# Neighbourhood attention on Trainium2: unnormalised exponentials, the inverse sums spread by a product with the identity

## The reference

```python
q, k, v = jnp.split(h @ w_qkv, 3, axis=-1)            # 16 heads of 64
q, k = rms_norm_2(_heads(q), q_g), rms_norm_2(_heads(k), k_g)
# the same for the 256 context tokens: k_c, v_c
s_loc = einsum('bhrqd,bhrikd->bhrqik', qg, kg) * scale + bias    # 4 rows x 64 columns of the grid
s_loc = where(col_mask, s_loc, NEG_INF)
s_ctx = einsum('bhrqd,bhcd->bhrqc', qg, k_c) * scale
p = softmax(concatenate([s_loc, s_ctx], -1), -1)
o = einsum(p_loc, vg) + einsum(p_ctx, v_c)
x = x + g1 * (merge(o) @ w_o)
x = x + g2 * conv_ffn(modulate(x, ...), ...)
```

## Time and profile before

| | |
|---|---|
| timed runs | 1769.03, 1772.07, 1773.03 us |
| profiled execution, its own time | 1772.83 us |
| its span, first to last instruction | 1771.0 us |
| mean granted TensorE clock | 0.969 |
| busy, share of the span | TensorE 95%, weight loads 83%, VectorE 56%, ScalarE 42%, GpSimd 5% |
| neighbourhood attention, first scores to first product of the projection | 1464.09 to 1541.72 us |

### The profile page before, as it was taken

How to read it: one execution, slowest core, us unless ns; L and a number is a source line. 1 busy time by engine, 2 the same in 40 slices (tenths; PEclk the granted TensorE clock), 3 DMA queues, 4 the chain that set the end, 5 groups by cost and what they waited for, 6 DMA issues and landing times.

```text
span 1771.0 us, 29417 instructions
## 1 busy us (share of the span) xinstructions
PE 1677.8 (95%) x11903; PEld 1469.2 (83%) x11903; DVE 999.2 (56%) x1209; ACT 751.0 (42%) x1104; POOL 91.1 (5%) x70
## 2 busy tenths in 40 slices
PE   6999999999999999779989999999979998789998
PEld 6998998989999989777767888888858874589998
DVE  6777556558785565553356443443352328776664
ACT  5545544445445544453234322233242324555453
POOL 0110000001100000020011000000020102110000
PEclk9999999999999999879999999999979998989999
DMA  7675665766665657512122323332324322045654
GB/s 250 224 232 198 203 212 191 239 221 199 233 211 198 210 173 246 199 38 82 48 72 75 92 82 100 115 90 68 93 72 149 94 83 46 20 139 169 202 175 122
DMA packets 329969, 259.69 MB, mean 147 GB/s; under 512 B 24017, under 2 KB 322385, under 8 KB 329826
## 3 DMA queue, kind: packets, MB, share of 16 engines
q1 hardware_dynamic: 311184, 251.55, 44.2%
q10 hardware_dynamic: 18642, 6.18, 1.7%
HBM read 256.65 MB, written 1.05 MB: 146 GB/s over the span
## 4 chain that ended last, share of the span: by engine, by line
PE 82%; DVE 9%; ACT 5%; issue 2%; DMA 1%; POOL 1%; ACTq 0%; SPq 0%; DVEq 0%
PE banks_g L1018 40%; PE banks_g L768 20%; PE banks_g L758 4%; PE banks_g L1006 3%; PE banks_g L790 2%; PE bank_s L885 1%; ACT near_p L1592 1%; PE banks_g L750 1%; ACT w_hi L1223 1%; PE bank_m L804 1%; DVE near_p L2012 1%; DVE near_max L2179 1%; DVE w_lo L1731 1%; PE bank_t L898 1%; POOL h L1670 1%
## 5 line engine op out<-in xcount | busy, mean ns | idle before, releaser
L1018 PE MATMUL banks_g<-h_hi,w_lo 128*128 128x512 f32 (+1 forms) x864 | 299.9, 347 | 9.7 <-DVE h_lo L2115 9.7
L1018 PE MATMUL banks_g<-h_hi,w_hi 128*128 128x512 f32 (+1 forms) x864 | 297.9, 345 | 0.0
L1018 PE MATMUL banks_g<-h_lo,w_hi 128*128 128x512 f32 (+1 forms) x864 | 297.9, 345 | 0.0
L1985 DVE TENSOR_TENSOR w_lo<-raw,w_hi 128x2048 fp32r<-128x2048 f32 (+1 forms) x100 | 208.0, 2080 | 158.8 <-ACT w_hi L1386 158.7
L1731 DVE TENSOR_TENSOR w_lo<-raw,w_hi 128x2048 fp32r<-128x2048 f32 x92 | 210.7, 2290 | 94.9 <-ACT w_hi L1223 94.7
L768 PE MATMUL banks_g<-h_hi,w_lo 128*128 128x256 f32 x800 | 227.9, 285 | 0.0
L768 PE MATMUL banks_g<-h_hi,w_hi 128*128 128x256 f32 x800 | 223.3, 279 | 0.0
L768 PE MATMUL banks_g<-h_lo,w_hi 128*128 128x256 f32 x800 | 223.2, 279 | 0.0
L1386 ACT ACTIVATE w_hi<-raw 128x2048 fp32r<-128x2048 f32 (+1 forms) x100 | 173.3, 1733 | 74.3 <-DMA raw<-w_down 48.1
L1018 PEld LDWEIGHTS banks_g<-h_hi,w_lo 128*128 128x128 f32 x864 | 164.5, 190 | 33.6 <-DVE h_lo L2115 12.0
L1223 ACT ACTIVATE w_hi<-raw 128x2048 fp32r<-128x2048 f32 x96 | 183.0, 1906 | 6.9 <-DMA raw<-even_in 2.6
(11 more groups left out here) (313 smaller groups left out, 2948.3 us busy)
## 6 DMA issues: line engine op xcount, KB each, us to landing
raw<-w_in SPq DMA_DIRECT2D x76, 1024.0 KB, 4.9
ada_raw<-ada_w SPq DMA_DIRECT2D x48, 1024.0 KB, 7.2
raw<-w_up SPq DMA_DIRECT2D x88, 512.0 KB, 4.5
raw<-w_down SPq DMA_DIRECT2D x32, 704.0 KB, 4.4
raw<-w_branch SPq DMA_DIRECT2D x12, 1024.0 KB, 4.9
raw<-qkv SPq DMA_DIRECT2D x12, 1024.0 KB, 4.9
raw<-w_out SPq DMA_DIRECT2D x8, 1024.0 KB, 5.1
raw<-even_in SPq DMA_DIRECT2D x6, 1024.0 KB, 5.2
```

The source lines that it names most:

```text
L1018: last = nc.tensor.matmul(gb[:, m * SEQ:m * SEQ + nt], w[:, c, m0:m0 + P], a[:, c, 0:nt], start=c == 0 and n == 0, stop=c == kcs - 1 and n ...
L1985: nc.vector.tensor_tensor(w_lo[:, u % SLOTS, 0:n], raw[:, u % SLOTS, 0:n], w_hi[:, u % SLOTS, 0:n].bitcast(F32), ALU.subtract).then_inc(dv ...
```

## The change

The exponentials stay unnormalised. The scale goes into the queries' root (their root becomes sqrt(sum + 64 EPS), which folds 1/8 in), the bias is added in place in PSUM, maximum and exponential read PSUM, and the exponential's output is what is transposed. The reciprocals of the sums (128 queries on partitions, two heads) are spread by TensorE behind the values: a product of near_inv, broadcast to 64 columns, with the identity, for each head on its half, into columns 128 to 255 of the same bank. ScalarE copies the spread to SBUF (near_ib), VectorE multiplies the values by it (near_o), and high and low part are taken from near_o in a new entry, near split, one iteration later. The scores of step b wait for the exponential of step b-2; the exponential of step b waits for the transposes of step b-3. The products of scores and values themselves stay as they were.

```diff
--- before.py
+++ after.py
@@ -323,12 +323,14 @@
         for i in range(4):
             order.append(("unit", kind, i))
             order += between.get(f"{kind}{i}", [])
-    for b in range(19):
+    for b in range(20):
         if b < 16:
             order.append(("near scores", b))
         if 2 <= b <= 17:
             order.append(("near turn", b - 2))
-        if b >= 3:
+        if b >= 4:
+            order.append(("near split", b - 4))
+        if 3 <= b <= 18:
             order.append(("near values", b - 3))
         if b < 16:
             order.append(("near exp", b))
@@ -398,6 +400,7 @@
         mod = sb("mod", [P, DEPTH, 48, 2])
         s_cols = sb("s_cols", [P, KC, 32])
         eps = sb("eps", [P, 1])
+        eps_hd = sb("eps_hd", [P, 1])
         x_t = sb("x_t", [P, KC, SEQ])
         base = at[0]
 
@@ -504,7 +507,9 @@
         window = sb("window", [P, SEQ], offset=f_lo_at + 16384)
         near_max = sb("near_max", [P, 2, 2], offset=f_lo_at + 18432)
         near_sum = sb("near_sum", [P, 2, 2], offset=f_lo_at + 18464)
-        near_inv = sb("near_inv", [P, 2], offset=f_lo_at + 18496)
+        near_inv = sb("near_inv", [P, 4, 2], offset=f_lo_at + 18496)
+        near_o = sb("near_o", [P, 2, P], offset=f_lo_at + 18560)
+        near_ib = sb("near_ib", [P, 2, P], offset=f_lo_at + 19584)
         near_p = [sb(f"near_p{n}", [P, 2, 512], offset=h2_hi_at + 4096 * n) for n in range(3)]
         near_pt = sb("near_pt", [P, 2, 4, 2, P], offset=h2_hi_at + 12288)
         bias = [sb(f"bias{n}", [P, 4, SEQ], offset=c_t_at + 4096 * n if n < 2 else h2_hi_at + 20480)
@@ -1123,7 +1128,7 @@
 
                         pe.wait_ge(act_steps, act_.at(f"empty{END_JOBS[('nv', 3, 1)]}"))
                     if b >= 2:
-                        pe.wait_ge(dve_steps, dve_.at(f"near masked{b - 2}"))
+                        pe.wait_ge(act_steps, act_.at(f"near exp{b - 2}"))
                     for e in range(2):
                         r = slice(64 * e, 64 * e + 64)
                         last = nc.tensor.matmul(near_banks(b)[:, e, :], q_n[r, c, qt * P:qt * P + P], k_n[r, c, :],
@@ -1131,7 +1136,7 @@
                     last.then_inc(pe_steps, pe_.step(f"near scores{b}"))
                 elif what == "near turn":
                     b, = arg
-                    pe.wait_ge(dve_steps, dve_.at(f"near probs{b}"))
+                    pe.wait_ge(act_steps, act_.at(f"near exp{b}"))
                     for hf in range(2):
                         if b:
                             pe.wait_ge(act_steps, act_.at(f"near turned{b - 1} {hf}"))
@@ -1146,13 +1151,18 @@
                     qt, c = divmod(b, KC)
                     pe.wait_ge(act_steps, act_.at(f"near turned{b} 1"))
                     if b >= 2:
-                        pe.wait_ge(dve_steps, dve_.at(f"near lo{b - 2}"))
+                        pe.wait_ge(dve_steps, dve_.at(f"near o{b - 2}"))
                     ob = bank_o if b % 2 == 0 else bank_g[0]
                     for kt in range(4):
                         for e in range(2):
                             hh = 2 * c + e
-                            last = nc.tensor.matmul(ob[64 * e:64 * e + 64, 0:P], v_n[:, kt, hh * HD:hh * HD + HD],
-                                                    near_pt[:, b % 2, kt, e, :], start=kt == 0, stop=kt == 3)
+                            nc.tensor.matmul(ob[64 * e:64 * e + 64, 0:P], v_n[:, kt, hh * HD:hh * HD + HD],
+                                             near_pt[:, b % 2, kt, e, :], start=kt == 0, stop=kt == 3)
+                    pe.wait_ge(dve_steps, dve_.at(f"near inv{b}"))
+                    for e in range(2):
+                        last = nc.tensor.matmul(ob[64 * e:64 * e + 64, P:2 * P],
+                                                near_inv[:, b % 4, e:e + 1].to_broadcast([P, HD]), ident[:, :],
+                                                start=True, stop=True)
                     last.then_inc(pe_steps, pe_.step(f"near values{b}"))
                 elif what == "finish":
                     pe.wait_ge(dve_steps, dve_.at(f"empty{len(END_JOBS) - 1}"))
@@ -1573,8 +1583,9 @@
                     if half:
                         nt = SEQ if x == "q" else 512
                         act.wait_ge(pe_steps, pe_.at(f"sumsq{x}1"))
-                        nc.scalar.activation(m_root[0:16, 0:nt], bank_m[0:16, 0:nt], ACT.Sqrt, scale=1.0 / HD,
-                                             bias=eps[0:16, 0:1]).then_inc(act_steps, act_.step(f"root{x}"))
+                        by, e_ = (1.0, eps_hd) if x == "q" else (1.0 / HD, eps)
+                        nc.scalar.activation(m_root[0:16, 0:nt], bank_m[0:16, 0:nt], ACT.Sqrt, scale=by,
+                                             bias=e_[0:16, 0:1]).then_inc(act_steps, act_.step(f"root{x}"))
                 elif what == "qk spread":
                     x, = arg
                     if x == "k":
@@ -1588,8 +1599,11 @@
                         act.wait_ge(dve_steps, dve_.at(f"near masked{b - 1}"))
                         load_bias(b // 2 + 2)
                     act.wait_ge(dve_steps, dve_.at(f"near max{b}"))
+                    if b >= 3:
+
+                        act.wait_ge(pe_steps, pe_.at(f"near turn{b - 3} 1"))
                     for e in range(2):
-                        nc.scalar.activation(near_p[b % 3][:, e, :], near_p[b % 3][:, e, :], ACT.Exp,
+                        nc.scalar.activation(near_p[b % 3][:, e, :], near_banks(b)[:, e, :], ACT.Exp,
                                              bias=near_max[:, b % 2, e:e + 1], accum_out=near_sum[:, b % 2, e:e + 1]
                                              ).then_inc(act_steps, act_.step(f"near exp{b}"))
                 elif what == "near turn":
@@ -1602,12 +1616,17 @@
                                                                              act_.step(f"near turned{b} {hf}"))
                 elif what == "near values":
                     b, = arg
-                    qt, c = divmod(b, KC)
                     act.wait_ge(pe_steps, pe_.at(f"near values{b}"))
                     ob = bank_o if b % 2 == 0 else bank_g[0]
+                    nc.scalar.activation(near_ib[:, b % 2, :], ob[:, P:2 * P], ACT.Copy
+                                         ).then_inc(act_steps, act_.step(f"near ib{b}"))
+                elif what == "near split":
+                    b, = arg
+                    qt, c = divmod(b, KC)
+                    act.wait_ge(dve_steps, dve_.at(f"near o{b}"))
                     nc.scalar.activation(
                         f_hi[:, 0:4, :].rearrange("p a (b t) -> p (a b) t", b=2)[:, c, qt * P:qt * P + P],
-                        ob[:, 0:P], ACT.Copy).then_inc(act_steps, act_.step(f"near hi{b}"))
+                        near_o[:, b % 2, :], ACT.Copy).then_inc(act_steps, act_.step(f"near hi{b}"))
                 elif what == "finish":
                     for b in range(4):
                         t, c4 = divmod(b, 2)
@@ -1622,6 +1641,7 @@
             enter("start")
             pool.sem_inc(pool_steps, pool_.total("layer") or 1)
             nc.gpsimd.memset(eps[:, :], EPS).then_inc(pool_steps, pool_.step("eps"))
+            nc.gpsimd.memset(eps_hd[:, :], EPS * HD).then_inc(pool_steps, pool_.step("eps"))
             nc.gpsimd.memset(ones[:, :], 1.0).then_inc(pool_steps, pool_.step("ones"))
             nc.gpsimd.memset(logf[:, :, :], 0.0).then_inc(pool_steps, pool_.step("logf"))
             nc.gpsimd.memset(s_cols[:, :, :], 0.0).then_inc(pool_steps, pool_.step("s cols"))
@@ -2004,14 +2024,11 @@
                                         f_hi[:, i % (FC // 2), 0:n].bitcast(F32), ALU.subtract
                                         ).then_inc(dve_steps, dve_.step(f"f lo{ly} {i}"))
 
-            def near_normalize(b):
+            def near_reciprocal(b):
 
                 dve.wait_ge(act_steps, act_.at(f"near exp{b}"))
-                nc.vector.reciprocal(near_inv[:, :], near_sum[:, b % 2, :]).then_inc(dve_steps, dve_.step("near inv"))
-                own()
-                nc.vector.tensor_tensor(near_p[b % 3][:, :, :], near_p[b % 3][:, :, :],
-                                        near_inv[:, :].rearrange("p (e o) -> p e o", o=1).to_broadcast([P, 2, 512]),
-                                        ALU.mult).then_inc(dve_steps, dve_.step(f"near probs{b}"))
+                nc.vector.reciprocal(near_inv[:, b % 4, :], near_sum[:, b % 2, :]).then_inc(
+                    dve_steps, dve_.step(f"near inv{b}"))
 
             u = 0
             for what, *arg in END:
@@ -2164,30 +2181,33 @@
                 elif what == "near scores":
                     b, = arg
                     qt, c = divmod(b, KC)
-                    pb, sbk = near_p[b % 3], near_banks(b)
+                    sbk = near_banks(b)
                     dve.wait_ge(pool_steps, pool_.at(f"windowed{b // 2}"))
 
                     dve.wait_ge(pe_steps, pe_.at(f"near scores{b}"))
```

(25 more changed lines are left out.)

## The result

The changed kernel takes 1743.62 us (median of 4 runs, 1743.26 to 1747.49), the kernel before 1771.84 us beside it (1769.03 to 1773.03): ratio 0.9846, 95% interval 0.9834 to 0.9859. The sign and the mechanism in the stage were as forecast; about ten microseconds come from a place that the prediction had priced at nothing.

A forecast was written before the change was run, and what follows sets the result against it. The attention stage was bound by a VectorE and ScalarE chain of 4.27 us a step; TensorE at 3.49 would take over. The projection moves from 1541.72 to 1527.7, so 1772.07 - 14.0 = 1758.1 us, range 1751.5 to 1765.0.

The forecast's parts named there:

- the mechanism in the stage: Neighbourhood attention: a shorter VectorE and ScalarE chain leaves TensorE as bound, the step falling from 4.27 to 3.49 us.
- the bound moves from VectorE's chain to TensorE: Neighbourhood attention, per step: TensorE 3.49 us against at most 3.25 for ScalarE and 2.76 for VectorE.
- The prices taken from neighbouring rows: VectorE in the attention step: in-place addition 0.69 us, at most twice that; maximum from PSUM 1.22.
- TensorE's step: Attention step on TensorE: 3.11 us plus 0.38 for the added spread makes 3.49.
- the lower bound, 0.21: Spread product on TensorE: four records of 0.054 us each, without a gap; upper bound 0.75 a step.
- the half clock: Start of the attention stage: TensorE at half clock costs 2.5 us, bounds 0 and 4.9.
- the tail's 0.1: From the last spread to the projection: result, four short steps and a last 0.14, forecast 1.58 us.
- What follows is bound by its own work and moves as a whole.: Behind the attention stage: durations unchanged, so the stage's 14.0 us gain passes through whole.
- ScalarE's queue: Rival, attention steps: five pairs of bias transfers exposed, 6.5 us come back, 1764.6 us; chance 0.17.
- The added product: Rival, attention steps: the spread runs beside the values' end, step stays 3.11, 6.1 us more gained, 1752.0; chance 0.14.
- The step was shortened: Answers a rival: slow in-place addition keeps VectorE's attention step at 4.27 us, time 1772; chance 0.03.
- TensorE didn't stay at half clock: Answers the slower rival: half clock through the whole attention stage costs 51 us, 1809 us; chance 0.04.

The follow-up runs named there:

- after's: The changed kernel, all parts of the change made, against the kernel before: 1743.62 us; run again unedited for a second profile, 1744.05 us.

## Why the prediction was right and wrong

**Right: the bound moves from VectorE's chain to TensorE.** The chain of waits, the missing idle time and the steps of 3.11, 3.33 and 3.55 show it. The prices taken from neighbouring rows held: addition in place 0.698 for 0.69 (the upper bound was twice that), maximum 1.224 for 1.22, third scores 5.78 us after the first for 5.76 forecast (1466.33 - 1460.55), behind the last spread 1520.47 - 1519.03 = 1.44 for 1.58. By the Trainium skill, "VectorE: DVE Perf Modes", the section on the TRN2 errata, a PSUM source costs 62 cycles more than an SBUF one. The prediction made 0.13 us a step of it for addition and maximum together. That reading was wrong: the addition read PSUM before the change too, so the section charges the maximum alone, 0.065 us by its clock of 0.96 GHz (an estimate). The trace has 0.004 for it (1.224 for 1.220) and disagrees. The section says nothing of a PSUM destination; the addition grew from 0.681 to 0.695 and 0.698.

**Right in sign, wrong in size: TensorE's step.** "It stands behind a wait of its own, met long before, but a group behind waits starts 0.17 after the one before: 0.38 in all." What was measured is next to the lower bound, 0.21: 0.22 in the experiments. The 0.17 is there once between values and scores, with or without a spread in between; I charged it a second time. 16 x (0.38 - 0.22) = 2.6 us.

**Wrong in size: the half clock.** I took 2.5 us for it. From the third scores to the end of the last spread is 1519.03 - 1466.33 = 52.7; at full clock the groups add up to 14 x 1.06 + 16 x (1.02 + 1.03 + 0.22) = 51.2. So 1.5, which fits the one stretch of 3.4 us at half clock. That the clock would be half without a break until it came back for good was wrong for the kernel before as well: there it was full from 1469.4 to 1472.8. With the tail's 0.1 these make the stage 3.7 us shorter than forecast, 59.92 for 63.6.

**Wrong: "What follows is bound by its own work and moves as a whole. The queries' other scale and epsilon are one instruction for one, the extra memset on GpSimd lies beside the first loads."** This is the step that failed. The epsilon was priced as an instruction; it is also an allocation, and it moves every buffer behind it. That is 10.3 us of the 28.2 (1753.92 to 1743.62), and it acts ahead of the stage too, where the prediction had its first addition at 1466.29 "as now": 5.2 us ahead and 5.0 behind, over twelve profiles, in stages whose work the change leaves as it was. With the buffers held in place the kernel takes 1753.92, inside the range and 4.2 from the forecast, of which the two sizes above are 3.7.

The rivals: ScalarE's queue does hold the exponentials, but not TensorE. The added product is not hidden (0.22 a step). The step was shortened, and TensorE didn't stay at half clock. None of the rivals held the placement of the buffers.

**Open.** That the allocation causes the gain outside the stage is shown; why the relative place of two operands in SBUF changes the pace of products is not. No rule that I can state covers the table: at one placement the 256-column products ran near 113.5 in one group and near 118 in the next, and after's projection at 113.8 in one execution and 118.2 in another. What chooses between the two is open. Which bits of the distance count, and whether the other of the two weight parts or the transfers written into SBUF at the time have a share, was not tried.

## What to carry to other kernels

When the bound of a stage is a chain over two engines, take the normalisation out of it: apply the inverse to the product's small output instead of its large input, and let the engine that rests carry the spread. Sum each engine's whole step first, so that the next bound is known (here TensorE at 3.33 against 4.27).

Read a diff for what it allocates as well as for what it runs. Ahead of crediting an unexpected gain to an edit, make the kernel before with the same addresses, and the edit with the old ones: two kernels separate them. Profile each of them more than once: here the marks of one kernel moved by up to 3.7 us. In a kernel that lives on TensorE, a pad of 32 or 64 bytes between weights and streamed operands is worth a sweep of its own, stage by stage, once everything else is done.

## What the runs showed of the hardware

- The start-to-start time of TensorE's fp32r products at full clock depended on where the operands lie in SBUF: 226.7 to 234.3 ns with 512 columns. With 256 it was 113.4 to 120.4, and at one placement it also changed from execution to execution. A shift of 32 bytes was worth 10 to 15 us of 1772, and one of 64 cost 4. In the Trainium skill, "TensorE: Matmul & The Clock Gate", the section on the back-to-back issue gap gives the gap of a single product as a function of the number of columns and the clock alone, with 262 cycles for 256 columns (an estimate of 109 ns) and 518 for 512 (216 ns). Every row here is above it, by 4 to 10%, and by more or less with the placement. For a stream of weight loads and products the same section has about 131 ns with 512 columns; no row here comes near that.
- A wait that is already met added no gap of its own between values and spread. From values over spread to scores it is 0.93 + 0.32 = 1.25: twenty records of 0.054, and the 0.17 once, as without the spread.
- ScalarE's copy of 128 elements took 0.285 us out of PSUM and 0.329 out of SBUF (the high part), which read PSUM before (0.274); the exponential of 512 was 0.69 to 0.70 out of PSUM and 0.715 out of SBUF.
- VectorE reading and writing one PSUM bank in place costs hardly more than PSUM to SBUF: 0.695 and 0.698 against 0.681 for 128x512.
